# Experts' stage of a two-block transformer kernel: the first step's rows gathered on their own, and the steps and the weight ring reordered

## The chip, the cores and the metric

One core of one Trainium2 chip runs the whole program. The metric is device time in microseconds (us), of one execution from start to end; the median of three runs of the kernel before is 2145.59 us (2143.97 to 2146.25). An execution under the hardware profiler gave the trace that is read below.

## The reference

512 tokens of 1024 numbers pass through a first block (a recurrent layer, a sparse attention layer, two feed-forward layers) and then a second (retention and window attention merged, a mixture of experts, a gate). The change lies in the mixture of experts alone:

```python
# per token: the best of 4 groups, in it the best 2 of 8 experts (32 experts in all)
combine = sum(one_hot(expert_id) * (g_w * top_p))
for grp in range(4):
    hid = silu(h @ w_gate[e]) * (h @ w_up[e])      # 1024 -> 256, each of 8 experts
    y  += (hid * combine[e]) @ w_down[e]           # 256 -> 1024
```

Each token is needed by 2 of the 32 experts, so there are 1024 pairs of a token and an expert. An expert's weights are 3 MB (gate and up 2 MB, down 1 MB), of all 32 some 100 MB.

## The kernel before

**Routing and rows.** After the router, VectorE finds each pair's expert and its place `at` in a list of the 1024 pairs sorted by expert (`start` holds where each expert's pairs begin, `count` how many it has). TensorE turns the normalised tokens so that a token is one row (`nat`), and GpSimd stores them to DRAM (`token_rows`, 4 stores). From `at`, VectorE builds one-hot matrices (`slot_lane`, `slot_tile`) and TensorE multiplies them (L1369), which gives `slot_row`: for each of the 1024 places the token that stands there. GpSimd then gathers all 1024 rows in 8 indirect DMAs of 128 rows each (`rows_a`, `rows_b`, L3250). TensorE turns each of the 8 tiles (8 transposes of 128x128, L1380), ScalarE (L2067) and VectorE (L3060) copy one half each into `xs`, where all the sorted rows lie side by side.

**Steps.** The work is in 24 steps. A step handles two blocks of up to 64 rows, one in each half of the array (`half_of(0)`, `half_of(1)`). A "main" step takes the first 64 rows of expert n and of expert n + 16; there are 16. An "over" step takes rows past the 64th, for experts that have more than 64; there are 8, so 16 blocks, filled from block 0 on (block j stands in step j of half 0 for j under 8). A block that isn't needed is computed all the same, but its weights are not loaded: the indices of its indirect DMA lie out of bounds. The order is main, over, main, eight times over (`STEPS`).

For each step, ScalarE and VectorE copy a window of 64 columns of `xs` into `xw` (`window_a`, `window_b`; the start is read from `window_at`); TensorE makes gate and up (`up(s)`, 32 matmul records, L1413); ScalarE's Silu (L2081) and VectorE's product (L3072) give `xhid`; TensorE turns it (`turn_hid(s)`), ScalarE copies it to `xturn`, TensorE makes the down product (`down_moe(s)`, 16 records, L1437), ScalarE copies it to `y_out`, and GpSimd scatters its rows to DRAM (`store_y(s)`). TensorE's order is up(0), up(1), turn 0, down(0), turn 1, and then for s from 2 on: up(s), down(s - 1), turn_hid(s).

**Weights.** A "panel" is 1 MB of weights. SyncE loads the 96 panels of the main steps into a ring of 9 buffers in the order of `PANEL_ORDER` (per main step 4 for up, then 2 for down; L621). Nine are loaded ahead, while the router runs. Load n waits until TensorE has used panel n - 9. The over steps' panels come by indirect DMAs that GpSimd issues (`load_over(q)`, L3230; q = 3 * over step + 0 or 1 for the two halves of up, + 2 for down). Each q is two DMAs, one for each half, and there are two buffers for each half, used by turns, so `load_over(q)` waits until the product with q - 2 is done:

```python
if q >= 2:
    pool.wait_ge(over_used, 2 * q - 2)
```

TensorE waits for both halves of a panel. All of GpSimd's DMAs are issued in the order of its program: before, at each over step s, load_over(3o + 2), load_over(3o + 3), store_y(s - 1), load_over(3o + 4), store_y(s), store_y(s + 1).

Between stages TensorE computes filling products (`keep(b, n)`, L648) into a bank that nobody reads.

## Time and profile before

| | |
|---|---|
| median of 3 runs | 2145.59 us |
| the profiled execution, own time | 2143.46 us |
| its span in the trace | 2141.6 us |
| PE (TensorE matmul) busy | 2095.6 us, 98% |
| DVE (VectorE) busy | 1267.6 us, 59% |
| ACT (ScalarE) busy | 836.0 us, 39% |
| POOL (GpSimd) busy | 271.3 us, 13% |
| moved by DMA | 298.13 MB |
| experts' steps (first up to last down) | 1791.88 to 2062.82 us |

In rows by stretch the columns are: from and to, its length, then busy time (and instructions) of PE, PEld, DVE, ACT and POOL, the granted clock, the DMA share and GB/s. In rows in order of time: start, time taken, engine, line, what; in brackets how long the engine had been idle and what ended that.

PE counts as busy from a matmul's start to its modelled end, so 98% does not say that PE is what limits a stage. Busy time of PE includes the filling products. The DMA share of a stretch is the mean over the core's 16 DMA engines. All times in rows are microseconds from the span's start.

### The profile page before, as it was taken

To read this page: it belongs to the slowest core of one execution; us is meant where nothing else is said; L and a number is where in the kernel's file an instruction comes from. 1 tells how busy PE (TensorE), PEld (TensorE's weight loads), DVE (VectorE), ACT (ScalarE), POOL (GpSimd) and SP (SyncE) were. 2 spreads that over 40 slices of the span, in tenths; PEclk is the share of its full clock that TensorE was granted. 3 is DMA by queue.
4 is the path that set the end of the run, shared out by engine and by line. 5 is a ranking of instruction groups with operands and counts; after the bars stand their busy time and mean duration, and the time that the engine had idled before them with its cause. 6 is when DMAs were issued, how large, how long until landed. Compare 5 with 4: busy or idle time off the path is not lost.

```text
span 2141.6 us, 27223 instructions
## 1 busy us (share of the span) xinstructions
PE 2095.6 (98%) x10474; PEld 1578.0 (74%) x10474; DVE 1267.6 (59%) x1704; ACT 836.0 (39%) x1258; POOL 271.3 (13%) x234
## 2 busy tenths in 40 slices
PE   8999999999999999999999999999999998999998
PEld 6787788888878877888888888877778884333346
DVE  7887855555587678875655555588775454000038
ACT  6556522222253445774422222264552232122143
POOL 1334200000010064000100000020000023222220
PEclk9999999999999999999999999999999999999999
DMA  5322322223214352112322222221122158999961
GB/s 204 123 95 73 118 97 100 88 88 118 78 64 155 124 170 79 36 40 89 131 99 104 91 88 93 93 71 62 65 99 90 68 232 323 418 414 398 395 235 60
DMA packets 62622, 298.13 MB, mean 139 GB/s; under 512 B 14080, under 2 KB 14464, under 8 KB 34582
## 3 DMA queue, kind: packets, MB, share of 16 engines
q1 hardware_dynamic: 42560, 261.60, 31.9%
q0 software_dynamic: 19552, 34.55, 5.2%
q8 instruction: 63, 1.03, 0.2%
q10 hardware_dynamic: 416, 0.70, 0.1%
q14 instruction: 31, 0.25, 0.0%
HBM read 326.37 MB, written 22.48 MB: 163 GB/s over the span
## 4 chain that ended last, share of the span: by engine, by line
PE 79%; DVE 9%; DMA 6%; ACT 3%; issue 2%; POOL 1%; POOLq 0%; ACTq 0%; DVEq 0%
PE psum L652 21%; PE psum L654 21%; PE psum L653 21%; PE psum L1413 5%; DMA panel<-w_m 4%; PE psum L1437 3%; PE psum L1102 2%; PE psum L1077 1%; DVE a_lo L2137 1%; ACT a_hi L1520 1%; DMA over_panel<-w_m,over_row 1%; DVE xc L2294 1%; DVE hs L2248 1%; ACT hn_hi L1547 0%; PE psum L1235 0%
## 5 line engine op out<-in xcount | busy, mean ns | idle before, releaser
L652 PE MATMUL psum<-hn_hi,a_hi 128*128 128x512 f32 (+1 forms) x1592 | 628.4, 395 | 1.9 <-DVE a_lo L2126 0.9
L654 PE MATMUL psum<-hn_hi,a_lo 128*128 128x512 f32 (+1 forms) x1592 | 618.7, 389 | 0.0
L653 PE MATMUL psum<-hn_lo,a_hi 128*128 128x512 f32 (+1 forms) x1592 | 618.4, 388 | 0.0
L652 PEld LDWEIGHTS psum<-hn_hi,a_hi 128*128 128x128 f32 (+1 forms) x1592 | 297.2, 187 | 74.0 <-issue 8.2
L653 PEld LDWEIGHTS psum<-hn_lo,a_hi 128*128 128x128 f32 (+1 forms) x1592 | 297.4, 187 | 64.8 <-issue 2.4
L654 PEld LDWEIGHTS psum<-hn_hi,a_lo 128*128 128x128 f32 (+1 forms) x1592 | 297.0, 187 | 64.3
L2137 DVE TENSOR_TENSOR a_lo<-a_raw,a_hi 128x2048 fp32r<-128x2048 f32 (+2 forms) x108 | 247.3, 2290 | 69.4 <-ACT a_hi L1520 68.9
L1520 ACT ACTIVATE a_hi<-a_raw 128x2048 fp32r<-128x2048 f32 (+2 forms) x108 | 201.4, 1866 | 71.0 <-PE psum L654 61.8
L2236 DVE TENSOR_TENSOR h<-h,psum 128x512 f32<-128x512 f32 x176 | 119.4, 687 | 78.4 <-PE psum L654 78.4
L3150 POOL TENSOR_TENSOR sq<-sq 128x512 f32<-128x512 f32 x5 | 7.8, 1555 | 1121.6 <-ACT sq L1533 1121.6
L3072 DVE TENSOR_TENSOR xhid<-xsg,psum 128x256 f32<-128x256 f32 x24 | 10.1, 422 | 231.3 <-ACT xsg L2081 231.3
L1701 ACT ACTIVATE sg<-sg 128x512 f32<-128x512 f32 x44 | 27.8, 633 | 286.3 <-DVE sg L2407 286.3
L652 PE MATMUL psum<-hid_hi,b_hi 128*128 128x512 f32 x352 | 137.3, 390 | 2.2 <-DVE h L2236 2.1
L654 PE MATMUL psum<-hid_hi,b_lo 128*128 128x512 f32 x352 | 137.0, 389 | 0.0
L653 PE MATMUL psum<-hid_lo,b_hi 128*128 128x512 f32 x352 | 137.0, 389 | 0.0
L1413 PE MATMUL psum<-panel,xw 128*64 128x512 f32 x512 | 113.4, 595 | 0.0
L2412 DVE TENSOR_TENSOR hid<-sg,psum 128x512 f32<-128x512 f32 x44 | 30.3, 688 | 113.8 <-PE psum L654 113.6
L1703 ACT ACTIVATE hid_hi<-hid 128x512 fp32r<-128x512 f32 x44 | 27.8, 632 | 177.5 <-DVE hid L2412 177.5
L1527 ACT ACTIVATE b_hi<-b_raw 128x1024 fp32r<-128x1024 f32 x64 | 67.0, 1051 | 65.4 <-PE psum L654 63.2
L1413 PEld LDWEIGHTS psum<-panel,xw 128*64 128x64 f32 x512 | 35.3, 137 | 66.9 <-issue 66.5
L2143 DVE TENSOR_TENSOR b_lo<-b_raw,b_hi 128x1024 fp32r<-128x1024 f32 x64 | 79.8, 1254 | 1.0 <-ACT b_hi L1527 1.0
L652 PEld LDWEIGHTS psum<-hid_hi,b_hi 128*128 128x128 f32 x352 | 66.1, 188 | 17.5 <-issue 2.6
(533 smaller groups left out, 3257.2 us busy)
## 6 DMA issues: line engine op xcount, KB each, us to landing
a_raw<-w_a SPq DMA_DIRECT2D x115, 1024.0 KB, 5.1
panel<-w_m SPq DMA_DIRECT2D x96, 1024.0 KB
b_raw<-w_b SPq DMA_DIRECT2D x64, 512.0 KB, 3.4
q_scratch<-q_hi POOLq DMA_DIRECT2D x7, 384.0 KB
q_scratch<-qb_lo POOLq DMA_DIRECT2D x7, 384.0 KB
q_hi<-q_scratch POOLq DMA_DIRECT2D x7, 384.0 KB
q_lo<-q_scratch POOLq DMA_DIRECT2D x7, 384.0 KB
token_rows<-nat POOLq DMA_DIRECT2D x4, 512.0 KB, 5.4
```

The source lines that it names most:

```text
L652: pe.matmul(out, w_hi, x_hi, start=first, stop=False)
L653: pe.matmul(out, w_hi, x_lo, start=False, stop=False)
L654: return pe.matmul(out, w_lo, x_hi, start=False, stop=last)
L1102: mm = pe.matmul(bank[6 + at % 2][side * DV:(side + 1) * DV, t * P:(t + 1) * P], w, x, start=i == 0, stop=i == len(steps) - 1)
L1413: mm = pe.matmul(bank[v][rows, :], xw[:, v, k, rows], w[half][:, k % 4 * 2 * EFF:(k % 4 + 1) * 2 * EFF], start=k == 0, stop=k == KT - 1)
L1437: mm = pe.matmul(bank[4 + 2 * v + hb][rows, :], xturn[:, v, f * P + half * SLOTS:f * P + (half + 1) * SLOTS], w[half][:, f * D + hb * 512: ...
L1520: act.activation(a_hi[s % 2][:, 0:w], a_raw[s % 2][:, 0:w], ACT.Copy).then_inc(a_rounded, 1)
L1527: act.activation(b_hi[s % 2][:, :], b_raw[s % 2][:, :], ACT.Copy).then_inc(b_rounded, 1)
L2137: V.tensor_tensor(a_lo[s % 2][:, 0:w], a_raw[s % 2][:, 0:w], a_hi[s % 2][:, 0:w], ALU.subtract) \
L2143: V.tensor_tensor(b_lo[s % 2][:, :], b_raw[s % 2][:, :], b_hi[s % 2][:, :], ALU.subtract) \
L2236: V.tensor_tensor(h[:, m, :], h[:, m, :], bank[4 + m % 4][:, :], ALU.add).then_inc(y_free, 1)
L2412: V.tensor_tensor(hid[:, f, :], sg[:, f, :], ps[1][:, :], ALU.mult).then_inc(tile_free, 2)
```

## The change

- `STEPS` begins with main 0, main 1, over 0 in place of main 0, over 0, main 1. The rest of the order stays: main, over, main.
- `PANEL_ORDER`: the down panels of step 0 come right behind its up panels, ahead of the up panels of the next main step.
- The first step's 128 rows (64 of expert 0 and 64 of expert 16) get a gather of their own. VectorE makes `first_lane` (a comparison of 128x512 for each half) from `at`; TensorE multiplies it with the token numbers (8 products of one column); the result `slot_first` drives one indirect DMA into `rows_first`, ahead of the eight. Its 8 transposes are copied by ScalarE straight into `xw`.
- TensorE's order becomes: transposes of `rows_first`, up(0), the eight tiles' transposes (with turn_hid(0) before the seventh), down(0), up(1), turn 1, and from s = 2 on as before.
- Filling products: 12 become 5 and 1, and the 6 behind the transposes go.
- On GpSimd the first two over loads wait for 3 and 5 turned tiles rather than for all 8; the load of `ptr` (for a later stage) stands behind all tiles; stores and over loads follow the new step order.
- The gathered tiles lie in other buffers (`rows_d`, `rows_c`, and `rows_b` has 2 in place of 4).
- A Silu on a small tile is added right behind the router's Exp on ScalarE.

```diff
-STEPS = [(kind, n) for o in range(XOVER // 2) for kind, n in (("main", 2 * o), ("over", o), ("main", 2 * o + 1))]
+STEPS = [("main", 0), ("main", 1), ("over", 0)] + [
+    (kind, n) for o in range(1, XOVER // 2) for kind, n in (("main", 2 * o), ("over", o), ("main", 2 * o + 1))]
...
-        if s and STEPS[s - 1][0] == "main":
-            down_at[s - 1] = len(order)
-            order += [(STEPS[s - 1][1] + XHALF * half, 2) for half in range(2)]
+        d = 0 if s == 0 else s - 1
+        if s != 1 and STEPS[d][0] == "main":
+            down_at[d] = len(order)
+            order += [(STEPS[d][1] + XHALF * half, 2) for half in range(2)]
...
             keep(0, 8)
+            pe.wait_ge(place_ready, 1)
+            for k in range(2 * NT):
+                mm = pe.matmul(bank[2][:, 0:1], first_lane[:, k, :, :].rearrange("p h c -> p (h c)"), pr[:, 1, k:k + 1],
+                               start=k == 0, stop=k == 2 * NT - 1)
+            mm.then_inc(rank_mm, 1)
             for k in range(2 * NT):
                 if k % NT == 0:
-                    pe.wait_ge(place_ready, k // NT + 2)
+                    pe.wait_ge(place_ready, k // NT + 3)
...
-            keep(0, 12)
-
-            for a in range(PAIRS // P):
+            keep(0, 5)
+
+            pe.wait_ge(y_stored[0], 16)
+            for f in range(2):
+                for k in range(4):
+                    mm = pe.transpose(bank[4 + f][:, k * P:(k + 1) * P], rows_first[:, (4 * f + k) * P:(4 * f + k + 1) * P], ident)
+                mm.then_inc(xs_mm, 1)
+            keep(0, 1)
...
-            keep(0, 6)
...
             up(0)
+            for a in range(PAIRS // P):
+                if a == 6:
+                    turn_hid(0)
+                turn_rows(a)
+            down_moe(0)
             up(1)
-            turn_hid(0)
-            down_moe(0)
             turn_hid(1)
...
+            for f, ready in enumerate((xwa_ready, xwb_ready)):
+                act.wait_ge(xs_mm, f + 1)
+                act.activation(xw[:, 0, 4 * f:4 * f + 4, :], bank[4 + f][:, :].rearrange("p (k c) -> p k c", k=4), ACT.Copy) \
+                   .then_inc(ready, 1)
+            silu_x(0)
...
+            first_at, at_second = pr[:, 8, 0:1], pr[:, 9, :]
+            step(V.tensor_scalar(first_at, start[:, XHALF:XHALF + 1], float(LAST_WINDOW), None, ALU.min))
+            step(V.tensor_scalar(at_second, at, first_at, None, ALU.subtract))
+            for half, x in enumerate((at, at_second)):
+                lane = V.tensor_tensor(first_lane[:, :, half, :],
+                                       x.rearrange("p (k o) -> p k o", o=1).to_broadcast([P, 2 * NT, SLOTS]),
+                                       by_pair(cnc("iota", SLOTS), 2 * NT), ALU.is_equal)
+            lane.then_inc(place_ready, 1)
...
             for c in range(2):
+                if c:
+                    V.wait_ge(rank_mm, 2)
+                    V.tensor_copy(slot_first[:, :], bank[2][:, 0:1]).then_inc(tables_ready, 1)
...
             pool.wait_ge(tables_ready, 1)
+            pool.indirect_dma_start(rows_first[:, :], None, nat_dram, bass.IndirectOffsetOnAxis(ap=slot_first[:, 0:1], axis=0)) \
+                .then_inc(y_stored[0], 16)
+            pool.wait_ge(tables_ready, 2)
...
+            pool.wait_ge(tables_ready, 4)
+            pool.wait_ge(xs_mm, 2 + 2 * 3)
+            load_over(0)
+            pool.wait_ge(xs_mm, 2 + 2 * 5)
+            load_over(1)
+            pool.wait_ge(xs_mm, 2 + 2 * (PAIRS // P))
             pool.dma_start(ptr[:, :, :], p_t.rearrange("(k p) s -> p k s", p=P)).then_inc(table_loaded, 16)
-            pool.wait_ge(tables_ready, 3)
-            pool.wait_ge(xs_first, PAIRS // P)
-            pool.wait_ge(xs_second, PAIRS // P)
-            load_over(0)
-            load_over(1)
-            pool.wait_ge(tables_ready, 5)
...
+            over_at_step = [s for s in range(NSTEP) if STEPS[s][0] == "over"] + [NSTEP + 1]
+            at = 0
+            for o in range(XOVER // 2):
+                s, following = over_at_step[o:o + 2]
+                while at < s - 1:
+                    store_y(at)
+                    at += 1
+                load_over(3 * o + 2)
+                if o + 1 < XOVER // 2:
+                    load_over(3 * o + 3)
+                store_y(at)
+                at += 1
+                if o + 1 < XOVER // 2:
+                    load_over(3 * o + 4)
+                while at < following - 1:
+                    store_y(at)
+                    at += 1
```

## Rows read from the trace of the kernel before

**Rows 1.** Busy time by stretch, with granted clock, DMA share and GB/s last

```profile
...
1774.50:1788.50 14.00, 10.20 (x70) 8.14 (x69) 10.69 (x30) 4.07 (x7) 7.08 (x8) 1.00 0.96 336
1788.50:1793.20 4.70, 4.70 (x26) 3.26 (x26) 1.85 (x4) 2.72 (x4) 1.90 (x2) 1.00 0.13 20
1793.20:1850.00 56.80, 55.78 (x260) 18.37 (x258) 7.73 (x23) 10.96 (x20) 16.28 (x17) 1.00 1.01 413
1850.00:2041.00 191.00, 183.71 (x846) 60.64 (x844) 14.48 (x34) 39.36 (x68) 49.62 (x50) 1.00 1.00 405
```

**Rows 2.** DMA queues from 1640 to 2141: packets, MB, share of engines

```profile
...
q0 software_dynamic: 13456, 22.10, 12.6%
```

**Rows 3.** Who waited for whom, PE alone, 1740 to 2070

```profile
...
PE psum L1437 <- DMA panel<-w_m: 6.2, 5, 1.9
```

**Rows 4.** PE in order of time, 1740 to 1815: start, us, what

```profile
...
1777.29 1.09 PE L1380 MATMUL psum<-cn,rows_a 128*128 128x128 f32 x8 [0.23 <-DMA rows_a<-token_rows,slot_row]
...
1785.01 3.07 PE L1380 MATMUL psum<-cn,rows_b 128*128 128x128 f32 x24 [1.20 <-ACT xs L2067]
...
1789.19 2.75 PE L648 MATMUL psum<-cn 128*128 128x256 f32 x12
1791.88 7.09 PE L1413 MATMUL psum<-panel,xw 128*64 128x512 f32 x32
...
1802.94 3.65 PE L1413 MATMUL psum<-over_panel,xw 128*64 128x512 f32 x16 [0.54 <-DMA over_panel<-w_m,over_row]
```

**Rows 5.** PE in order of time, 1800 to 2066

```profile
...
1818.31 3.60 PE L1437 MATMUL psum<-over_panel,xturn 128*64 128x512 f32 x16
...
1822.21 7.09 PE L1413 MATMUL psum<-panel,xw 128*64 128x512 f32 x32
...
1833.03 7.09 PE L1413 MATMUL psum<-over_panel,xw 128*64 128x512 f32 x32
...
1843.85 7.09 PE L1413 MATMUL psum<-panel,xw 128*64 128x512 f32 x32
1852.05 3.65 PE L1437 MATMUL psum<-over_panel,xturn 128*64 128x512 f32 x16 [1.11 <-DMA over_panel<-w_m,over_row]
...
2032.45 3.65 PE L1437 MATMUL psum<-panel,xturn 128*64 128x512 f32 x16 [1.42 <-DMA panel<-w_m]
...
2059.17 3.65 PE L1437 MATMUL psum<-panel,xturn 128*64 128x512 f32 x16 [1.05 <-ACT xturn L2052]
```

**Rows 6.** GpSimd's DMA issues in order of time

```profile
...
1772.81 1.03 POOL L3250 DMA_INDIRECT rows_a<-token_rows,slot_row  x1 [6.34 <-DMA token_rows<-nat]
...
1794.94 0.99 POOL L3230 DMA_INDIRECT over_panel<-w_m,over_row  x1 [0.30 <-issue]
...
1822.75 1.01 POOL L3230 DMA_INDIRECT over_panel<-w_m,over_row  x1 [8.71 <-PE psum L1437]
1824.07 1.00 POOL L3230 DMA_INDIRECT over_panel<-w_m,over_row  x1 [0.31 <-issue]
```

**Rows 7.** VectorE in order of time, 1740 to 1815

```profile
...
1768.69 0.23 DVE L3004 TENSOR_TENSOR passed<-pr,cn 128x64 f32<-128x64 f32 x1
...
1769.82 1.29 DVE L3011 TENSOR_TENSOR slot_lane<-pr,cn 128x512 fp32r<-128x512 f32 x2
...
1799.46 0.42 DVE L3072 TENSOR_TENSOR xhid<-xsg,psum 128x256 f32<-128x256 f32 x1 [7.05 <-ACT xsg L2081]
```

**Rows 8.** ScalarE in order of time, 1740 to 1815

```profile
...
1777.98 0.60 ACT L2067 ACTIVATE xs<-psum 128x512 f32<-128x512 f32 x1 [10.71 <-PE psum L1380]
```

**Rows 9.** The chain that ended last, 1640 to 2141: start, us, what

```profile
...
1781.68 6.54 DMA rows_b<-token_rows,slot_row
...
1838.89 13.03 DMA over_panel<-w_m,over_row
```

**Rows 10.** Stretches around the fall of the granted clock

```profile
...
1450.00:1453.00 3.00, 0.67 (x11) 0.52 (x12) 2.81 (x2) 2.99 (x4) 0.00 (x0) 1.00 0.00 0
1453.00:1457.00 4.00, 4.00 (x21) 2.69 (x17) 3.59 (x5) 2.51 (x2) 0.00 (x0) 0.57 0.01 2
```

More of the change, by code:

```diff
@@ L260, in build @@
             vcz = sb("vcz", [P, GROUPS, HPG, DV], F32, st)
+        with ExitStack() as st:
+            sb("under_rows_c", [P, S], F32, st)
+            rows_c = sb("rows_c", [P, D], F32, st)
         sd = sb("sd", [P, S])
@@ L324, in build @@
             rows_a = sb("rows_a", [P, NT, D], F32, st)
+            with ExitStack() as s2:
+                rows_first = sb("rows_first", [P, D], F32, s2)
+                rows_d = sb("rows_d", [P, D], F32, s2)
             sb("over_rows_a", [P, NT, D], F32, st)
@@ L356, in build @@
             slot_row = sb("slot_row", [P, PAIRS // P], I32, st)
+            slot_first = sb("slot_first", [P, 1], I32, st)
+            ROWS = [rows_a[:, 0, :], rows_a[:, 1, :], rows_d[:, :], rows_a[:, 2, :], rows_a[:, 3, :],
+                    rows_b[:, 0, :], rows_b[:, 1, :], rows_c[:, :]]
             held = sb("held", [P, 4, XBLOCKS], F32, st)
@@ L1410, in up @@
                         w, used = weights(s, k // 4)
+                    if s == 0 and k == 4:
+                        pe.wait_ge(xwb_ready, 1)
                     for half in range(2):
@@ L1429, in down_moe @@
                 pe.wait_ge(xturn_done, s + 1)
+                if s == 0:
+                    pe.wait_ge(xs_first, PAIRS // P - 1)
+                    pe.wait_ge(xs_second, PAIRS // P - 1)
+                if s == 1:
+                    pe.wait_ge(xs_first, PAIRS // P)
+                    pe.wait_ge(xs_second, PAIRS // P)
                 if s >= 2:
@@ L2040, in _ @@
             act.activation(rt[:, 5, :], rt[:, 4, :], ACT.Exp).then_inc(small_out, 1)
+            act.activation(warm[:, 7:8], eps, ACT.Silu)
             def window_a(s):
@@ L2081, in _ @@
                 act.activation(xsg[:, v, :], bank[v][:, 0:EFF], ACT.Silu).then_inc(xgate_done, 1)
+            for f, ready in enumerate((xwa_ready, xwb_ready)):
[3 more added lines that the diff above has]
+            silu_x(0)
+            for a in range(PAIRS // P):
+                if a == 6:
+                    copy_turned(0)
+                act.wait_ge(xs_mm, 2 * a + 3)
+                act.activation(xs[:, 0:4, a * P:(a + 1) * P],
+                               bank[4 + 2 * a % 4][:, :].rearrange("p (k c) -> p k c", k=4), ACT.Copy).then_inc(xs_first, 1)
+            act.wait_ge(tables_ready, 3)
+            act.wait_ge(xs_first, PAIRS // P)
+            act.wait_ge(xs_second, PAIRS // P)
+            window_a(1)
+            window_a(2)
+            copy_y(0)
+            for s in range(1, NSTEP):
+                silu_x(s)
                 if s + 2 < NSTEP:
                     window_a(s + 2)
-                if s:
+                if s >= 2:
                     copy_y(s - 1)
-                    copy_turned(s)
+                copy_turned(s)
             copy_y(NSTEP - 1)
@@ L3072, in _ @@
                 V.tensor_tensor(xhid[:, v, :], xsg[:, v, :], bank[v][:, EFF:2 * EFF], ALU.mult).then_inc(xhid_done, 1)
+            gated(0)
+            for a in range(PAIRS // P):
+                V.wait_ge(xs_mm, 2 * a + 4)
+                V.tensor_copy(xs[:, 4:8, a * P:(a + 1) * P],
+                              bank[5 + 2 * a % 4][:, :].rearrange("p (k c) -> p k c", k=4)).then_inc(xs_second, 1)
+            V.wait_ge(tables_ready, 3)
+            V.wait_ge(xs_first, PAIRS // P)
+            V.wait_ge(xs_second, PAIRS // P)
+            window_b(1)
+            window_b(2)
+            rows_held()
+            for s in range(1, NSTEP):
+                gated(s)
                 if s + 2 < NSTEP:
                     window_b(s + 2)
-                if s == 0:
-                    rows_held()
             s, v = NSTEP - 1, (NSTEP - 1) % 2
```

53 lines of the change are left out of this document (13 added, 40 removed).

## The prediction

> **What bounds the kernel now.** I first looked at busy time by stretch around the experts' stage [rows 1]. From 1793.2 us on the DMA engines' share is 1.01 and then 1.00, with 405 to 413 GB/s: the reader is to see that weights stream without a pause. Just before lies a hole: in 1788.5 to 1793.2 the share is 0.13. The ring is full there, and nothing is freed until up(0) has used its first panels.
>
> Next, who waited for whom [rows 3]: TensorE waited for main panels 5 times, 6.2 us in all, and 1.11 us for an over panel [rows 5], together 7.3 us; the last of these ends at 2032.45. Behind it TensorE has work without a pause, but for 1.05 us at the very end [rows 5]. So two chains run almost level. The stream sets the end at present, and TensorE would be 7.3 us earlier if panels never came late.
>
> Then the order of time on TensorE. A step costs 10.82 us from one up to the next (1833.03 - 1822.21) [rows 5], of which up takes about 6.95 and down with the turn 3.9. The first transposes start at 1777.29, up(0) at 1791.88 [rows 4], up(3) at 1822.21 and up(4), the second over step, at 1833.03 [rows 5].
>
> Last, how many over blocks are real: GpSimd's queue moved 22.10 MB from 1640 to 2141 [rows 2]. Four stores and eight gathers of rows, `ptr` and the eight gathers at the end are 21 transfers of 0.52 MB, 11.0 MB; the small store of 192 KB adds 0.2 and the scattered rows (1024 + 48 of 4 KB) 4.4. That leaves 6.5 MB, six panels: blocks 0 and 1 are real, in over steps 0 and 1, both in half 0.
>
> **The first step's start.** VectorE gets two small operations and two comparisons of 128x512 ahead of L3004, at 1768.69 [rows 7]. Small ones come at about 0.2 us each (an estimate from the 0.23 us one there), the two comparisons take 1.29 us. That is 1.7 us before `slot_tile`, and with the copy of `slot_first` 1.9 us for `slot_row`. `slot_first` itself is ready at about 1768.7 + 1.7 + 1.1 (L3004 to L3011) + 0.65 + 0.2 = 1772.4. The first gather went out at 1772.81 and waited for the stores of rows until then [rows 6], so it is hardly later: 1773.0. Its landing is as before (1777.29 - 1772.81 = 4.5): transposes from 1777.5, 1.1 us, with ScalarE's two copies of 0.60 [rows 8] half beside them, up(0) at 1779.0. That is 12.9 us earlier. The eight gathers begin at 1774.3 in place of 1772.81, and the last, 6.54 us from issue to landing [rows 9], lands at some 1790 to 1792 beside the first panels.
>
> **What of it stays on TensorE.** Up(0) ends at 1786.1. Only then come the eight tiles. Three of them took 3.07 us [rows 4], so eight take 8.2, which lay partly under the gathers before and now lie alone; with the turn 8.6, to 1794.7. The filling products (2.75 us for 12 [rows 4]) are gone. Down(0) ends at 1798.3, up(1) at 1805.3. Its turn follows at once, so Silu and product show: from up(0)'s end at 1798.97 to the product's end at 1799.88 they took 0.9 us [rows 4, 7]; with the turn, up(2) starts at 1806.8 and up(3) at 1817.6. Before, it was 1822.21: of 12.9 us 4.6 are left.
>
> **What the new order puts on the path.** Over 0 is now step 2, over 1 still step 4. load_over(4), the second half of over 1's up, reuses the buffer of down(2). Before, down(1) read it and ended at 1821.91; the two issues began 0.84 and 2.16 us later [rows 5, 6], and the panel was needed at 1833.03 + 3.5 = 1836.5, 14.6 us after. Now down(2) ends at 1828.05, TensorE's next work is up(4), and it needs the panel at 1831.9, 3.9 us after. Behind this wait stand up(4)'s second half, down(3) and all that follows.
>
> The second issue goes out at 1830.2. Its landing has no row of its own. Below: 8.0 us, from 1794.94 to the end of the wait at 1802.94, when few panels were in the queue [rows 4, 6]. Above: 12.4 us, since at 1836.5 nobody waited for what was issued at 1824.07, and 13.03 us for the next such panel [rows 6, 9]. I take 10.0, between them, as the queue then is shorter than at 1838 (the stream is ahead) but not empty. So the panel is there at 1840.2, TensorE waits 8.3 us, and up(5) starts 7.6 us later, at 1847.8, 3.95 us later than before (1843.85). The over panel for down(4), waited for at 1852.05, is then early enough. If no other panel came late, TensorE would end 3.95 - 7.3 = -3.35 us against before. With the bounds of 8.0, 12.4 and 13.03 us: -5.3, -0.95 and -0.35.
>
> The Trainium skill (DMA: Bandwidth & Descriptors, Anatomy of one DMA) puts such a transfer at 2.0 us plus bytes over 436 GB/s, 4.4 us for this panel. By it TensorE would wait 2.7 us and end 8.95 us earlier, with the end then left to the stream; the rows of 8 to 13 us speak against it, as two queues share the engines.
>
> **What of it stays in the stream.** The hole is worth 4.7 x 0.87 = 4.1 us, and 14 x 0.04 = 0.56 us were idle during the gathers: 4.65 [rows 1]. Panels 9 to 12 are freed at 1782.6 and 1786.1, not 1795.5 and 1799, and the first real over panels from 1789 on, so the hole is filled. From 1776 to 1847 gathers, panels 9 to 24, six over panels and `ptr` are queued, enough to keep the engines busy at 413 GB/s. Against it: 0.52 MB more to move (1.3 us at 413 GB/s, 1.56 at 336; I take 1.4), 0.2 us later start, 0.2 us between first gather and the rest, 0.4 us idle during the gathers. Lead: 4.65 - 1.4 - 0.2 - 0.2 - 0.4 = 2.45 us; bounds 3.35 (only the bytes) and 1.2 (a whole issue of 1.3 us more between the gathers). Down panel 87 at 2032.45 comes that much earlier, and so does the end. The ring could run dry at 1847: down(3) frees panels 3.9 us later than before. With the lead of 2.45 the stream must have had 6.4 us of queued loads at 1843.5; the share of 1.01 says that it had some, not how many.
>
> The Trainium skill says the same against the change (same page, Issuing engines are not separate DMA queues): transfers from whichever engine run on the same 16 DMA engines and interleave. By that rule, the trace agrees, loads moved beside gathers gain only the hole.
>
> **Edits at nothing.** The added Silu's table load lies where ScalarE idles 10.71 us before 1777.98 [rows 8]; the one that it spares lay under up(0), so it would cost or save nothing either way. The changed order on GpSimd past step 5 is as before. VectorE's tables end 1.9 us later, at about 1783.4, while it waits for up(0)'s Silu until 1786.5. `ptr` is bytes moved about in the same stream.
>
> **The sum.** The stream gives -2.45, TensorE -3.35; the later one counts: -2.45, rounded to -2.5 us. The profiled execution took 2143.46 us (span 2141.6), so 2141.0 on that footing; it lies 2.1 us below the median of the runs. From the median of 2145.59: **2143.1 us**. About 0.2%, 4.3 us, is what a measurement of this kernel can tell from no change, and the forecast is inside it.
>
> **Rivals.**
> - *The stream isn't the limit* (0.15). If panels ahead of time are worth more than the hole, TensorE's chain alone counts: -5.3 us with a landing of 8.0, 2140.3 us; with no wait for the over panel at all 4.35 + 7.3, 2133.9 us. For it: TensorE waits only 7.3 us in 270. Against: a share of 1.00 over 191 us.
> - *Slower: the over panel for up(4) lands late* (0.12). It gains nothing from 13.4 us after issue on and each us more is a us more; slower by 0.2% from 17.7 us on: 2149.9 us. If the ring runs dry as well, the same lateness counts fully in the stream, at most +3.9 at 10 us landing, 2149.5 us. For it: 13.03 us were seen [rows 9], beside stores in the same queue. Against: only 1 MB real in it.
> - *The start isn't earlier* (0.07): the first gather lands late or in the eight's company, and up(0) starts some 3 us after my time or more. Then the late panel takes what is left: about 2145.6 us.
> - Inside the forecast (0.66) lies the clock. TensorE idles some 2.4 us at 1775.1 to 1777.5, with 6 in place of 18 filling products around it. It granted 0.57 over 1453 to 1457, after a stretch with 0.67 of 3 us busy [rows 10], which is 3.4 us at 1.2 rather than 2.4 GHz. During up(0) it would cost 1.7 us on TensorE: -3.35 becomes -1.65, 2143.9 us. I give it 1 in 4.
>
> **Range and chances.** 2139.6 to 2147.4 us takes in the bounds of landing and lead, the clock, half of the first rival, and the smaller prices of the second; some 2 in 10 are left out. Faster by over 0.2%: 0.18 (first rival, and a little of the forecast's edge). Slower by over 0.2%: 0.13. Within: 0.69.
>
> **What would show it.** Right: up(0) near 1779, up(3) near 1817.6; no hole in the DMA share from 1776 to 1847; a wait of about 8 us for an over panel in the middle of up(4); waits for main panels down from 6.2 us to 1 to 2. Wrong: no such wait (then TensorE is early and the stream alone counts), a wait over 11 us or a hole at 1847 (then little or nothing is gained), a granted clock under 1.00 in 1776 to 1787, or step times other than 10.82 us.

## The result and the profile after

The change costs 3.2 us by the medians: 2147.29 us (median of 10 runs, 2146.76 to 2150.78) against 2144.13 (10 runs, 2141.10 to 2146.25), a ratio of 1.0021 with a 95% interval of 1.0013 to 1.0029 (the quotient of the two medians is 1.0015, inside that interval). Forecast were 2143.1 us, 2.5 us less than before, and no difference that can be told. The measured time lies just inside the stated range (up to 2147.4), but by luck: the three runs of before that the range was built on had a median 1.5 us above that of the ten. Against the kernel before the forecast was off by 5.7 us and had the wrong sign. The profiled execution took 2147.27 us (span 2145.5).

Where the time went is read best inside the experts' stage. I measure it from the first product of the expert ranks (L1362 before, L1374 after) to the end of the last down product: 298.1 us before, 303.5 after, so 5.4 us more. The spans differ by 3.9 only, since all ahead of the stage was 1.7 us earlier in this profile: the fall of the granted clock at 1453 us [rows 10] isn't there in it. The same product of rq and rk started at 1461.53 before and at 1459.81 after. The same two stretches in the profile after (columns as in [rows 1]):

```profile
1450.00:1453.00 3.00, 0.66 (x13) 0.63 (x12) 2.94 (x2) 2.99 (x4) 0.00 (x0) 1.00 0.00 0
1453.00:1457.00 4.00, 4.00 (x26) 3.00 (x21) 3.93 (x5) 2.39 (x2) 0.00 (x0) 1.00 0.01 2
```

With it the stage starts at 1763.04 in place of 1764.76, and times of before and after are compared below from that start on.

Busy time by stretch after, to be laid beside [rows 1]:

```profile
1774.50:1788.50 14.00, 13.79 (x82) 8.04 (x81) 9.36 (x28) 3.64 (x7) 6.75 (x7) 0.97 0.99 364
1788.50:1793.20 4.70, 3.65 (x34) 3.42 (x33) 2.76 (x4) 2.49 (x6) 3.74 (x4) 1.00 1.01 426
1793.20:1830.00 36.80, 33.12 (x153) 11.21 (x151) 7.57 (x22) 8.84 (x15) 8.23 (x10) 1.00 1.02 417
1830.00:1836.80 6.80, 4.94 (x12) 1.64 (x14) 0.00 (x0) 0.00 (x0) 1.89 (x2) 0.50 1.02 428
...
1840.30:1847.10 6.80, 4.30 (x11) 1.38 (x13) 0.00 (x0) 0.00 (x0) 0.81 (x1) 0.50 0.81 325
1845.00:1853.50 8.50, 8.50 (x36) 2.76 (x34) 0.85 (x2) 2.32 (x4) 1.99 (x2) 0.88 0.17 48
1853.50:2034.80 181.30, 179.34 (x830) 58.92 (x828) 14.47 (x34) 38.07 (x66) 49.47 (x49) 1.00 1.00 405
```

The reader is to see three things. The old hole in 1788.5 to 1793.2 is filled: a DMA share of 1.01 where it was 0.13. A new and larger one stands at 1845 to 1853.5, with 0.17: 8.5 x 0.83 = 7.1 us idle. And twice, for 6.8 us each, TensorE was granted only the lower of its two clock levels (0.50, 1.2 GHz). (The 0.97 in the first row comes from its start, under filling products; from 1776 to 1787 the granted clock was 1.00.)

Who waited for whom on PE, 1740 to 2070 (us in total, times, longest):

```profile
PE psum L1440 <- DMA over_panel<-w_m,over_row: 8.6, 2, 4.8
PE psum L1470 <- DMA panel<-w_m: 2.0, 1, 2.0
...
PE psum L1405 <- DMA rows_c<-token_rows,slot_row: 1.1, 1, 1.1
...
PE psum L1470 <- DMA over_panel<-w_m,over_row: 0.8, 1, 0.8
```

PE in order of time after (start, time taken, engine, line, what; in brackets the idle time ahead and what ended it):

```profile
1776.34 1.09 PE L1394 MATMUL psum<-cn,rows_first 128*128 128x128 f32 x8 [0.21 <-DMA rows_first<-token_rows,slot_first]
...
1777.80 7.09 PE L1440 MATMUL psum<-panel,xw 128*64 128x512 f32 x32
...
1816.17 7.09 PE L1440 MATMUL psum<-panel,xw 128*64 128x512 f32 x32
1824.09 3.65 PE L1470 MATMUL psum<-over_panel,xturn 128*64 128x512 f32 x16 [0.83 <-DMA over_panel<-w_m,over_row]
...
1831.86 6.12 PE L1440 MATMUL psum<-over_panel,xw 128*64 128x512 f32 x16 [3.75 <-DMA over_panel<-w_m,over_row]
1842.80 5.77 PE L1440 MATMUL psum<-over_panel,xw 128*64 128x512 f32 x16 [4.83 <-DMA over_panel<-w_m,over_row]
...
2034.49 5.35 PE L1470 MATMUL psum<-panel,xturn 128*64 128x512 f32 x16 [1.96 <-DMA panel<-w_m]
```

The first two rows are the start of the first step; up(3) is at 1816.17; the rows at 1831.86 and 1842.80 are the two halves of up(4), each behind a wait of its own, and each some 6 us long where such a half took 3.65 [rows 4]. The last row is the last panel that TensorE waited for, as at 2032.45 in [rows 5].

GpSimd's issues behind these waits, two for each over panel:

```profile
1813.24 0.99 POOL L3290 DMA_INDIRECT over_panel<-w_m,over_row  x1 [1.12 <-issue]
1814.54 0.99 POOL L3290 DMA_INDIRECT over_panel<-w_m,over_row  x1 [0.30 <-issue]
...
1828.54 1.01 POOL L3290 DMA_INDIRECT over_panel<-w_m,over_row  x1 [9.76 <-PE psum L1470]
1829.86 0.99 POOL L3290 DMA_INDIRECT over_panel<-w_m,over_row  x1 [0.31 <-issue]
```

The first pair is load_over(3), the first half of up(4)'s panels; the second pair load_over(4). The first issue of a pair is for half 0 and fetches 1 MB; the second, for half 1, fetches nothing in over steps 0 and 1, where only the blocks of half 0 are real. TensorE waits for both. The chain that ended last gives their landings:

```profile
1811.12 12.83 DMA over_panel<-w_m,over_row
...
1829.86 12.81 DMA over_panel<-w_m,over_row
```

12.8 us each from the second issue on, for load_over(2) and load_over(4), or 14.1 us from the first issue, the one with the bytes. load_over(3), issued between them at 1814.54, let up(4) start at 1831.86, 17.3 us later. All landings below are those of a pair, counted from its second issue, as the prediction did.

**The account.** From the stage's start, up(0) comes 14.8 us in, in place of 27.1: 12.4 earlier. Up(3) comes after 53.1 in place of 57.4: 4.3 earlier. Up(5) at 1852.31 comes after 89.3 in place of 79.1 [rows 5]: 10.2 later. So 14.5 us were lost between up(3) and up(5). Waits took 0.83 + 3.75 + 4.83 = 9.4 of it, and the two halves of up(4), 6.12 + 5.77 with nothing to wait for inside them, some 4.8 (a whole up takes 7.09): the granted clock fell at 1830.0 and at 1840.3, while TensorE was waiting, and each time stayed low into the half behind the wait. Meanwhile SyncE could load nothing, as no main panel was used up: its longest wait, for the release of a ring buffer, took 28.0 us (11.3 before, in the same window of 1796 to 1862). The ring ran dry, and the stream stood still from 1845 on. In the end the late stream ends the stage: the last wait for a main panel comes 271.5 us in, in place of 267.7, 3.8 later (the lead of 2.45 forecast less the 7.1 us of the new hole would be 4.65), and the down product behind that wait runs at the lower clock, 5.35 in place of 3.65. That makes 3.8 + 1.7 = 5.5 of the 5.4 us. TensorE's own chain accounts for less: without the last wait of 1.96 us and the 1.7 us behind it the stage would have ended 1.7 us later than before (an estimate, 5.4 - 2.0 - 1.7).

### The profile page after: what moved, and what is told of

Its sections match the earlier page's. It is cut to its first block, busy times and chain, and to the rows that moved or that the text cites. A ratio compares the mean times of both kernels' runs of the same rounds, so it can differ in the third digit from the quotient of the medians.

```text
span 2145.5 us, 27223 instructions
## 1 busy us (share of the span) xinstructions
PE 2098.0 (98%) x10474; PEld 1578.8 (74%) x10474; DVE 1268.8 (59%) x1708; ACT 837.0 (39%) x1260; POOL 272.1 (13%) x235
## 4 chain that ended last, share of the span: by engine, by line
PE 81%; DVE 9%; ACT 3%; DMA 3%; issue 2%; POOL 1%; POOLq 0%; ACTq 0%; DVEq 0%
PE psum L664 21%; PE psum L666 21%; PE psum L665 21%; PE psum L1440 6%; PE psum L1470 4%; PE psum L1114 2%; PE psum L1089 1%; DVE a_lo L2183 1%; DMA over_panel<-w_m,over_row 1%; DMA panel<-w_m 1%; ACT a_hi L1556 1%; DVE xc L2340 1%; DVE hs L2294 1%; DMA rows_c<-token_rows,slot_row 0%; ACT hn_hi L1583 0%
```

## The experiments

All times below are ratios to the kernel before on the same chip, in brackets their 95% intervals; "the stage" is measured as above (298.1 us before, 303.5 after). The first group of four was made to put the blame on the order, the gather or the clock.

**The over step third, in every triple.** The kernel after, with one regular order main, main, over, so that no two over steps are nearer than three steps:

```diff
-STEPS = [("main", 0), ("main", 1), ("over", 0)] + [
-    (kind, n) for o in range(1, XOVER // 2) for kind, n in (("main", 2 * o), ("over", o), ("main", 2 * o + 1))]
+STEPS = [(kind, n) for o in range(XOVER // 2) for kind, n in (("main", 2 * o), ("main", 2 * o + 1), ("over", o))]
```

> The changed kernel with one difference: every over step stands behind two main steps (main 2o, main 2o + 1, over o), so that a whole step lies again between the over step's down product and the next over panel that reuses its buffer. Theory A (the over panels 3 and 4 come late; the waits of 3.75 and 4.83 us at up(4), the two falls of the granted clock that follow them, 4.6 us, and the DMA hole of about 8 us at 1845 to 1853 are all their consequence): no wait for an over panel in up of the second over step above 1 us, no hole, no clock fall there, and the stream sets the end: 2.5 to 3 us under the kernel before, 5 to 7 us under the changed kernel, ratio 0.9986. Theory B (the own gather with its eight transposes behind up(0) is what costs): the time stays within 2 us of the changed kernel, ratio 1.001 to 1.002. Theory C (the clock falls come from the fewer filling products at the start, not from the waits): the falls stay, ratio about 1.000.

Measured: 2145.91 us, 1.0007 [0.9998, 1.0016], stage 301.0 us. The waits in up(4), the hole and both falls of the clock are gone. It is no faster than before all the same, so the expectation was missed. The stream now sets the end, and in another place. TensorE waited for main panels nine times, 11.1 us in all; two early waits and the last (read as the one at 2034.49 after):

```profile
1860.09 3.65 PE L1439 MATMUL psum<-panel,xw 128*64 128x512 f32 x16 [1.91 <-DMA panel<-w_m]
...
1877.38 3.65 PE L1469 MATMUL psum<-panel,xturn 128*64 128x512 f32 x16 [2.02 <-DMA panel<-w_m]
...
2046.45 3.65 PE L1469 MATMUL psum<-panel,xturn 128*64 128x512 f32 x16 [1.69 <-DMA panel<-w_m]
```

The last wait stands 19.5 us ahead of the stage's end, where it stood 30.4 ahead before (2062.82 - 2032.45). It is for down panel 93 of the 96 (93 and 87 counted from 0): six more panels must have come by then, 15.5 us of stream at 1.05 MB and 405 GB/s each, and 10.9 us less work stands behind. The difference, 4.6 us, is what the place of the last over step would cost; no run tests this working.

**The order of before, the rest of the change kept.**

```diff
-STEPS = [("main", 0), ("main", 1), ("over", 0)] + [
-    (kind, n) for o in range(1, XOVER // 2) for kind, n in (("main", 2 * o), ("over", o), ("main", 2 * o + 1))]
+STEPS = [(kind, n) for o in range(XOVER // 2) for kind, n in (("main", 2 * o), ("over", o), ("main", 2 * o + 1))]
```

> The changed kernel with the old order of steps: over 0 is the second step again; the own gather, the ring's order and the fewer filling products stay. Theory A: the late load of panel 4 is gone (the first real panels 0 and 1 are now needed at 1797 and 1800.5, and they landed at 1801.0 and 1808.7 in the changed kernel), so TensorE waits some 4 us twice in up(1) in place of up(4); frees come late too, a short hole near 1812 to 1818; 0 to 2 us over the kernel before. Theory B: ratio 1.001 to 1.002 as the changed kernel, with no wait of more than 2 us in up(1).

Measured: 2142.13 us, 0.9994 [0.9985, 1.0004]: better than I expected. The long waits that I feared in up(1) weren't there in its profile, but that shows little: TensorE came to up(1) late by itself, behind a wait of 2.66 us for the last gathered tile and a granted clock of 0.50 from 1797.1 to 1803.9, and this execution took 2145.88 us, 3.75 above the median. What the new order had cost is gone, and so is most of what the gather had won, since nothing certain is left against before.

**Filling products in the waits.** The kernel after, with 16 of them ahead of each half of up(4):

```diff
                     if k % 4 == 0:
+                        if s == 4:
+                            for _ in range(16):
+                                pe.matmul(bank[2][:, 2 * P:4 * P], ident, cn[:, CN["ident"]:CN["ident"] + 2 * P],
+                                          start=True, stop=True)
```

> The changed kernel with 16 filling products (3.7 us at 2.4 GHz) ahead of each half of up(4), just before TensorE waits for over panels 3 and 4. Theory A: the waits stay as they are in time of landing (the panels come at the same time), but TensorE is active during them, the granted clock stays at 2.4 GHz, and the 4.6 us that up(4)'s two halves took longer are saved in part: up(5) starts 2.5 to 4.6 us earlier, the time is 2 to 4 us under the changed kernel, about that of the kernel before. If the falls have nothing to do with the waits, up(4)'s halves take 6.1 and 5.8 us as before and the time stays.

Measured: 2149.84 us, 1.0029 [1.0017, 1.0042]. PE around up(4) (the rows of L1437 are the filling):

```profile
1831.74 7.07 PE L1437 MATMUL psum<-cn 128*128 128x256 f32 x32
1838.74 3.65 PE L1444 MATMUL psum<-over_panel,xw 128*64 128x512 f32 x16
1842.32 7.17 PE L1437 MATMUL psum<-cn 128*128 128x256 f32 x32
1849.43 3.65 PE L1444 MATMUL psum<-over_panel,xw 128*64 128x512 f32 x16
```

I had mis-sized the filling: 16 products leave 32 records and take 7.07 us, so they last longer than the waits, and no wait is left to be seen. The forecast gain didn't come, and the run can't price the clock. It does show that filling keeps the clock: both halves took 3.65 us. It also shows that the ring runs dry without any wait, if TensorE is only late: the DMA share was 0.03 from 1848 to 1856.

**The order alone.** The kernel before, with main, main, over throughout and the change's loop on GpSimd (its text stands in the diff ahead):

```diff
-STEPS = [(kind, n) for o in range(XOVER // 2) for kind, n in (("main", 2 * o), ("over", o), ("main", 2 * o + 1))]
+STEPS = [(kind, n) for o in range(XOVER // 2) for kind, n in (("main", 2 * o), ("main", 2 * o + 1), ("over", o))]
...
-            for s in range(NSTEP):
-                kind, o = STEPS[s]
-                if kind == "over":
...
+            over_at_step = [s for s in range(NSTEP) if STEPS[s][0] == "over"] + [NSTEP + 1]
...
```

> The kernel before with every over step behind two main steps, and GpSimd's issues in that order; no own gather, ring order as it follows from the steps. Tells how much of e1's time the new order gives by itself. Theory A: the hole at 1788.5 to 1793 stays, the stream sets the end, the waits of 0.5 us for over panels vanish but save nothing: within 1 us of the kernel before, ratio 0.9995 to 1.0005, and e1 is 2 to 3 us faster than this.

Measured: 2149.09 us, 1.0023 [1.0013, 1.0033], stage 304.5 us, against my expectation. Its last wait for a main panel:

```profile
2049.41 3.65 PE L1437 MATMUL psum<-panel,xturn 128*64 128x512 f32 x16 [1.60 <-DMA panel<-w_m]
```

So the regular order costs 5.1 us by itself; that it does so at the end is the working above, and not tested. Beside the first run it gives the price of the rest: the two have the same order, and with the gather of its own and its company the time is 3.2 us lower (2145.91 against 2149.09, on one chip; the two intervals overlap by 0.0003). That fits the lead of 2.45 us in the stream (bounds 1.2 to 3.35) that the prediction worked out; the run doesn't part the gather from the rest of the change.

The second group asks whether the late panels of up(4) alone explain the loss, and what the clock adds.

**Filling that fits.** As the filling above, with 7 and 14 products:

```diff
+                        if s == 4:
+                            for _ in range((7, 14)[k // 4]):
+                                pe.matmul(bank[2][:, 2 * P:4 * P], ident, cn[:, CN["ident"]:CN["ident"] + 2 * P],
+                                          start=True, stop=True)
```

> As the run with 16 filling products ahead of each half of up(4), but sized by what that run showed (0.44 us for one product, so 16 took 7.07 and 7.17 us and ended 4 us after panel 4 had landed at 1845.3): 7 products ahead of the first half (3.1 us, under the 3.75 us wait) and 14 ahead of the second (6.2 us). Theory A1 (the clock falls are a price of the waits that comes on top of them): the granted clock stays at 2.4 GHz at up(4), its halves take 3.65 us each, and the time is 2 to 4 us under the changed kernel, ratio to before 1.0000 to 1.0010. Theory A2 (the falls only fill time that TensorE would have waited anyway, since the stream and the late panels set the end): the falls go, the time stays within 1.5 us of the changed kernel, ratio 1.0014 to 1.0025.

Measured: 2147.89 us, 1.0018 [1.0009, 1.0027]. PE again:

```profile
1834.65 3.65 PE L1444 MATMUL psum<-over_panel,xw 128*64 128x512 f32 x16 [0.46 <-DMA over_panel<-w_m,over_row]
1838.24 6.31 PE L1437 MATMUL psum<-cn 128*128 128x256 f32 x28
1846.41 3.65 PE L1444 MATMUL psum<-over_panel,xw 128*64 128x512 f32 x16 [1.87 <-DMA over_panel<-w_m,over_row]
```

The clock stays at 1.00 and the halves at 3.65 us, and from up(3) to up(5) it takes 33.5 us in place of 36.1; yet the timed runs show no gain over the kernel after (1.0021 [1.0013, 1.0029]). The profile does: its stage is 300.7 us, 2.8 shorter. The two don't agree, so what the falls cost here lies between nothing and some 3 us. The hole in the stream stays:

```profile
1847.00:1854.50 7.50, 7.50 (x38) 2.83 (x36) 0.85 (x2) 1.97 (x4) 1.99 (x2) 1.00 0.23 76
```

So with the clock held up, late panels alone keep the kernel 0.18% over before.

**The order of before, filled.** The second run with 2 and 4 filling products ahead of tiles 7 and 8 of the gathered rows:

```diff
                 if a == 6:
                     turn_hid(0)
+                    keep(0, 2)
+                if a == 7:
+                    keep(0, 4)
                 turn_rows(a)
```

> The changed kernel with the old order of steps (over 0 second), and 2 and 4 filling products ahead of the seventh and eighth tile's transposes, where that kernel waited 0.53 and 2.66 us for gathered rows and the clock fell at 1797.1 for 6.8 us. If the fall there costs on the path: 1 to 2 us under the run without them (2142.13), so 2140 to 2141, ratio 0.9985 to 0.9990. If the stream alone sets the end: within 1 us of that run, ratio 0.9990 to 0.9996, and either way under the kernel before.

Measured: 2142.68 us, 0.9996 [0.9987, 1.0005]. With the old order over 0 comes early, and in this profile TensorE waits for its panels:

```profile
1803.05 3.65 PE L1439 MATMUL psum<-over_panel,xw 128*64 128x512 f32 x16 [2.61 <-DMA over_panel<-w_m,over_row]
1809.92 4.96 PE L1439 MATMUL psum<-over_panel,xw 128*64 128x512 f32 x16 [3.22 <-DMA over_panel<-w_m,over_row]
```

In this profile the earlier start is spent on waiting for over 0, and filling ahead of the tiles gains nothing (0.9996 against 0.9994 without it), which the expectation had as the case of the stream setting the end. The new place of over 0 takes the wait for over 0 away, and brings that of over 1.

**The late panel, put into the kernel before.** This is the test of the cause. Nothing of the change is in it; GpSimd only holds load_over(4) back until the down product of main 1 has read its panels:

```diff
                     store_y(s - 1)
+                    if o == 0:
+                        pool.wait_ge(main_used, DOWN_AT[2] + 2)
                     if o + 1 < XOVER // 2:
                         load_over(3 * o + 4)
```

> The kernel before with one over panel issued late: GpSimd issues load_over(4) only when down(2) is done, as the changed kernel must, some 10 us after the time of before (1833 rather than 1822.75); nothing else is changed. Theory A (that lateness is the changed kernel's loss): the panel lands at 1845 to 1847, TensorE waits 8 to 10 us in the middle of up(4), later waits for main panels shrink from 6.2 to under 2 us, the ring has a hole of some us at 1848 to 1856, and the time is 3 to 6 us over the kernel before, ratio 1.0014 to 1.0028. Theory B (own gather, transposes behind up(0)): no such loss, ratio 0.9998 to 1.0006.

Measured: 2149.48 us, 1.0024 [1.0015, 1.0034], stage 304.6: 5.6 us more than before. PE, and below it GpSimd:

```profile
1846.83 6.13 PE L1413 MATMUL psum<-over_panel,xw 128*64 128x512 f32 x16 [9.37 <-DMA over_panel<-w_m,over_row]
```

```profile
1834.35 1.01 POOL L3230 DMA_INDIRECT over_panel<-w_m,over_row  x1 [19.54 <-PE psum L1437]
1835.67 1.00 POOL L3230 DMA_INDIRECT over_panel<-w_m,over_row  x1 [0.31 <-issue]
```

And its stretches:

```profile
1841.60:1851.80 10.20, 4.97 (x12) 1.64 (x14) 0.00 (x0) 0.00 (x0) 0.37 (x1) 0.50 1.00 405
1851.00:1857.50 6.50, 6.50 (x30) 2.19 (x28) 0.85 (x2) 2.06 (x4) 1.98 (x2) 0.93 0.28 78
```

Here is the whole picture of after, made in the kernel before by one late issue: a landing 11.2 us after it, a wait of 9.4 us, 10.2 us at the lower clock, a half of up that takes 6.13 in place of 3.65, and right behind it the stream at 0.28. The last wait for a main panel comes 274.3 us into the stage in place of 267.7. The wait, the hole and the time were as expected. One thing the run doesn't separate: the two stores behind load_over(4) in GpSimd's program go out late with it (1836.97 and 1838.31 in place of 1825.37 and 1834.63).

**The short gap where nothing has to be loaded.** Two regular triples and then the old order, so that the short gap lies between over 1 and over 2, and over 2 isn't needed:

```diff
+STEPS = [(kind, n) for o in range(2) for kind, n in (("main", 2 * o), ("main", 2 * o + 1), ("over", o))] + [
+    (kind, n) for o in range(2, XOVER // 2) for kind, n in (("main", 2 * o), ("over", o), ("main", 2 * o + 1))]
```

> The changed kernel with the short gap between two over steps moved from over 0 / over 1 (both real) to over 1 / over 2: main 0, 1, over 0, main 2, 3, over 1, then main, over, main as before. The load that is now late is panel 7 of an over block that isn't needed, 9 to 12 us from its second issue to its landing even so, TensorE waits 5 to 8 us in the middle of up(7). Theory A: the loss by waiting is then 7 us against 7.3 us that the stream holds TensorE back anyway, no second over wait of 3.75 us, no hole in the stream: 0 to 3 us under the kernel before, ratio 0.9986 to 1.0000. If any wait of TensorE of that length at this place lets the ring run dry: 1 to 4 us over it.

Measured: 2146.91 us, 1.0014 [1.0005, 1.0023]. PE:

```profile
1865.47 3.65 PE L1440 MATMUL psum<-over_panel,xw 128*64 128x512 f32 x16
1876.13 6.64 PE L1440 MATMUL psum<-over_panel,xw 128*64 128x512 f32 x16 [7.01 <-DMA over_panel<-w_m,over_row]
```

A wait of 7.01 us for a pair of indirect DMAs that fetch no row at all (the second issue was at 1867.29, so 8.8 us to the end). The time is 3.0 us over before, and the ring did run dry, as the expectation's second case has it: the share was 0.25 from 1878 to 1888, 7.5 us idle, as much as in the kernel after. But the path is another. Behind this place TensorE never waits for a panel again, though it ends late: its own chain sets the end, no longer the stream, so the hole by itself costs nothing here. Each of the two rows has a part of the hole in it:

```profile
1871.90:1882.10 10.20, 5.97 (x14) 1.92 (x16) 0.00 (x0) 0.00 (x0) 0.37 (x1) 0.50 0.71 278
1882.10:2041.00 158.90, 158.90 (x736) 52.39 (x734) 12.79 (x30) 34.75 (x60) 43.48 (x43) 1.00 0.98 390
```

**The same, filled.** This made it the right place to price the clock (the expectation says that the stream had no hole there; it had the one of 7.5 us, which held nobody up). 14 filling products ahead of the second half of that up:

```diff
+                        if s == 7 and k == 4:
+                            for _ in range(14):
+                                pe.matmul(bank[3][:, 2 * P:4 * P], ident, cn[:, CN["ident"]:CN["ident"] + 2 * P],
+                                          start=True, stop=True)
```

> The run with the short gap between over 1 and over 2, and 14 filling products (0.44 us each, 6.2 us) ahead of the second half of up(7), where TensorE waited 7.01 us for a panel that isn't needed and the granted clock then stood at half for 10.2 us. In that run the stream had no hole and TensorE met no late panel afterwards, so TensorE's chain set the end. If the fall has a price of its own there: the halves take 3.65 us each, the time is 2 to 4 us under that run (2146.91), ratio to before 0.9995 to 1.0006. If not: the same as that run, 1.0010 to 1.0020.

Measured: 2143.97 us, 1.0004 [0.9995, 1.0013].

```profile
1869.44 6.31 PE L1437 MATMUL psum<-cn 128*128 128x256 f32 x28
1876.42 3.65 PE L1444 MATMUL psum<-over_panel,xw 128*64 128x512 f32 x16 [0.67 <-DMA over_panel<-w_m,over_row]
```

```profile
1871.90:1882.10 10.20, 9.53 (x46) 5.38 (x46) 0.91 (x2) 1.01 (x2) 1.72 (x2) 1.00 0.71 283
```

The panel lands as late as without the filling, but the half behind it takes 3.65 and not 6.64 us, and the kernel is faster by 2.9 us by the medians, 2.1 by the ratios (the two ran on different chips, and the two intervals overlap), and 2.7 by the stages (300.9 and 298.2). The timed runs alone leave the gain open. In the two profiles, though, TensorE waits for no panel behind this place, and the 3.0 us of the slow half come out at the stage's end but for 0.3: where TensorE's chain sets the end, a fall of the clock in a wait is paid nearly in full.

**The reader of the buffer earlier.** The kernel after, with down(2) right behind its own turn, so that the buffer of load_over(4) comes free ahead of up(3):

```diff
             for s in range(2, NSTEP):
                 up(s)
-                down_moe(s - 1)
+                if s != 3:
+                    down_moe(s - 1)
                 turn_hid(s)
+                if s == 2:
+                    down_moe(2)
```

> The changed kernel, steps in its own order, with one difference: down(2), the product that holds the buffer of panel 4, is computed right behind turn 2, ahead of up(3) and not behind it. Panel 4 is then issued some 7 us earlier (1821 to 1822 rather than 1828.5). Against it stand two short idle times of TensorE, 0.5 us before down(2) and 1.0 us before turn 3, since nothing lies between them any more. Theory A (the late reuse of one buffer is the loss): the wait of 4.83 us in the middle of up(4) falls under 2.5 us, that of 3.75 us at its start to about 2, the falls of the clock and the hole in the stream at 1845 to 1853 go, 3 to 5 us under the changed kernel, ratio to before 0.9990 to 1.0003. Theory B (own gather or the place of over 0 costs in itself): 1.0010 to 1.0020.

Measured: 2145.43 us, 1.0009 [1.0000, 1.0018], stage 300.1, better than after (the two intervals overlap) but not as good as hoped. Up(4) doesn't wait any more; down(2) does, whose own panel had never been early:

```profile
1827.29 5.07 PE L1470 MATMUL psum<-over_panel,xturn 128*64 128x512 f32 x16 [5.84 <-DMA over_panel<-w_m,over_row]
```

The wait of 9.4 us in all became one of 5.84, ahead of a product that the clock stretches to 5.07, and the hole became one of 4 us at a share of 0.34 (1831 to 1835).

**Two tries for a version that beats both.** The order of before with filling ahead of the tiles and, new, 5 and 6 products ahead of the halves of up(1):

```diff
+                        if s == 1:
+                            for _ in range((5, 6)[k // 4]):
+                                pe.matmul(bank[3][:, 2 * P:4 * P], ident, cn[:, CN["ident"]:CN["ident"] + 2 * P],
+                                          start=True, stop=True)
```

> A candidate for the best version: the changed kernel with the old order of steps, the filling products of the run before it (2 and 4 ahead of the seventh and eighth tile), and 5 and 6 more (2.2 and 2.6 us) ahead of the two halves of up(1), where that run waited 2.61 and 3.22 us for over panels and the granted clock then fell at 1809. If that fall, 1.3 us on the second half, stands on the path: 2141 to 2142, ratio 0.9985 to 0.9993. If the hole in the stream at 1813 to 1818 and the stream set the end: as that run, 2142.7, ratio 0.9993 to 0.9998.

Measured: 2143.18 us, 1.0000 [0.9991, 1.0009], slower than both cases of the expectation. And the order of before again as in the second run, same kernel, another chip:

> The same kernel as the run with over 0 as the second step again, on another chip, since its interval of 0.9985 to 1.0004 left open whether the own gather by itself gains. Expected the same: 1.5 to 2.5 us under the kernel before, ratio 0.9988 to 0.9995. If it comes out at 0.9998 or more, the own gather gains nothing that can be told.

Measured: 2143.73 us, 1.0000 [0.9991, 1.0009]. Its profile has the shortest stage of all (295.9 us), but the timed runs don't bear that out, and by the expectation's own sign (0.9998 or more) the gather gains nothing that can be told. No version beats the kernel before by more than the measurement can tell.

## Why the prediction was wrong

**The first step's start: right.** Up(0) came 12.4 us earlier, forecast 12.9; up(3) 4.3 earlier, forecast 4.6.

**What of it stays in the stream: right as far as it went.** The hole behind the gathers is gone, and the two kernels in one order differ by 3.2 us, forecast 2.45 within 1.2 to 3.35. (One term of the first rival doesn't agree with the text ahead of it, 4.35 where it had 4.6 us; nothing hangs on it.)

**What the new order puts on the path: the step that failed.** It had the right panel, the right reason (its buffer is read by down(2), 3.9 us ahead of its use) and the issue at 1830.2 (1829.86). What failed is the price it put on the late load: one wait of 8.3 us, with up(5) 3.95 us later and the stream untouched. Three terms of it were off.
- The landing. I took 10.0 us, because only 1 MB was real in GpSimd's queue; it took 12.8, near the upper end of my bounds (12.4 and 13.03). load_over(3) was in flight beside it until 1831.86, and the main panels kept the share at 1.02. The break-even that I had worked out stood at 13.4 us, but for this one panel alone.
- A second late panel that I never looked at. load_over(3) reuses the buffer of up(2)'s second half and goes out behind it, at 1814.54; I traced load_over(4) only. By the prediction's own times its second issue (1813.75 + 2.16 = 1815.9) lay 12.5 us ahead of up(4) at 1828.4, more than the 10.0 us that I took and less than my upper bound, so it deserved a term. It landed at the start of up(4) after 17.3 us and cost 3.75 us there, and 0.83 for down(2)'s panel came on top. In sum 9.4 us of waits, forecast 8.3. That the sum is so near is chance, since the wait in the middle was 4.83 and not 8.3: the first wait and the slow first half had let the second panel catch up.
- The clock. I gave it a chance in up(0), where nothing happened, and none in the waits that I forecast myself, though the row that I used for it [rows 10] shows a fall behind idle time. It fell in both waits, and the halves of up(4) took 4.8 us more; it fell once more behind the wait that ends at 2034.49, 1.7 us. The run with the gap later shows in its profile what such a fall costs where TensorE sets the end: 2.7 us of stage for one. In the kernel after, the filling runs leave it between nothing and 3 us.

Up(5) so came 10.2 us later instead of 3.95.

**The ring could run dry at 1847: what decided.** I had named it twice, and asked that the stream have 6.4 us of queued loads at 1843.5. It had less than it needed with TensorE 10.2 us late, and the share fell to 0.17 from 1845 on. That is the slower rival in its second form, where the lateness counts in the stream; I priced it at up to 3.9 us over before and gave it too little; measured are 3.2. The sum had taken the later of two chains, as if neither could move the other. The mistake in the weights was to treat landing, wait, clock and ring as separate small risks. They hang on each other: the late panel makes the wait, the wait makes the fall, both make TensorE free its buffers late, and the ring pays.

**That it is the late panels, and not the gather, is shown** from both sides: one held-back issue in the kernel before gives the same loss (1.0024), and the order of before takes the loss out of the kernel after (0.9994 and 1.0000 against 1.0021). A regular order that keeps the distance is no way out, as it costs 5.1 us (1.0023 in the kernel before). That the price of that order comes from its last step (4.6 us worked out) wasn't tested by itself. How the loss divides between load_over(3) and load_over(4) wasn't either. And why the gather's lead gains nothing with the order of before isn't settled: one profile shows waits of 2.61 and 3.22 us for over 0, the two of the unfilled kernel 1.75 us or less there and 2.0 and 2.7 for the last gathered tile.

The Trainium skill (DMA: Bandwidth & Descriptors, Anatomy of one DMA) gave the prediction its estimate of 4.4 us for the landing. No row bears that out for a DMA beside a saturated stream: a pair with 1 MB took 12.8 us (14.1 from its first issue), and a pair without a single row to fetch 8.8.

## What to carry to other kernels

When the order of steps changes, go through every buffer that two steps share and compare the distance between its last reader and its next use with the landing time under load, for all loads of the step and not just for the worst; two buffers by turns need an even spacing of their users. Where the margin is gone, count the lateness three times before calling it small: the wait, the clock behind the wait, and the buffers that the waiting engine frees late for another queue. And where two chains run level, moving one of them ahead is worth at most the slack of the other, so a gain of 12 us at a stage's start can be worth nothing at its end.

## What the runs showed of the hardware

- Indirect DMAs of which no row is fetched are not free beside a saturated stream (share 1.02): TensorE waited 7.01 us for a pair of them, 8.8 us from the second issue. Pairs of which one fetches 1 MB took 11.2 to 12.8 us, and 17.3 with another 1 MB issued just ahead.
- A hole in the weight stream costs only where the stream sets the end: one of 7.5 us, in the run with the gap later, was followed by no wait for a panel; the one of 7.1 us in the kernel after by one of 1.96 us.
- The granted clock fell to the lower level in waits of 3.75, 4.83 and 5.84 us and stayed there for 6.8 us, and in waits of 7.01 and 9.37 us for 10.2 us; filling products in the wait kept it at 1.00. For shorter ones the length alone doesn't tell: behind a wait of 2.02 us the product took 5.35 us in the run with the order of before (granted clock 0.58 from 1933 to 1937), and 3.65 in the run with the over step third; behind one of 1.96 us at 2034.49 it was 0.51 for 3.4 us.
